# Two small matrix products moved to where fillers ran, with new orders for weight halves, a table load and PSUM banks

## The chip, the cores and the metric

The kernel runs on one core of one Trainium2 chip. The core's engines are TensorE (PE, matrix products), VectorE (DVE), ScalarE (ACT), GpSimd (POOL) and the queue SyncE (SP) that issues the DMAs. The metric is the device time of one execution in microseconds (us). Lower is better. The time of the kernel before is 937.57 us, the median of three runs.

## The reference

All of it is fp32. A first transformer block works on 16 meta tokens and 256 tokens of width 1024 (two kinds of attention, a feed-forward with a causal convolution of width 3), a second on the 256 tokens (differential attention, retention, a feed-forward). What matters here is the frame around the two norms of the first block and the end of the second:

```python
# first block
h = h + rms_norm(mixed, norm_gains[layer, 1])
xn = rms_norm(h, norm_gains[layer, 2])
u = causal_depthwise_conv(xn @ w_up[layer], conv_w[layer], conv_b[layer])
u_gate, u_val = jnp.split(u, 2, axis=-1)
ffn = (jax.nn.gelu(u_gate, approximate=True) * u_val) @ w_down[layer]
h = h + rms_norm(ffn, norm_gains[layer, 3])
# second block: p is 256 tokens x 256, w_ple 256 x 1024
x = x + mixed @ w_out[i]
h2 = rms_norm_2(x, g_mlp[i])
x = x + jnp.square(jax.nn.relu(h2 @ w_ff1[i])) @ w_ff2[i]
gate_p = jax.nn.sigmoid(rms_norm_2(x, g_ple[i]) @ w_ple_gate[i])
x = x + gate_p * (p[i] @ w_ple[i])
return rms_norm_2(x, g_final)
```

The product `p @ w_ple` needs nothing that the two blocks compute. It is the "per-layer input" product that the change moves.

## The kernel before

Activations lie transposed, 8 tiles of 128 features by the tokens. Each fp32 matrix product is made of three products of halves: a value is split in a high half (rounded) and a low half (the rest), and high times high, high times low and low times high are summed in PSUM.

All weights lie in DRAM as one list of 285 blocks of 128x1024 in order of use. SyncE loads block i into one of four `raw` slots. ScalarE's `hi_to` (L826) makes its high half `wh`, VectorE's `lo_to` (L1270) its low half `wl`, and TensorE uses the block. In one of eight blocks (i % 8 == 7) VectorE makes the high half too, with a CAST (L1266). Four slots mean that the halves of block i can be made once block i-4 is used. `hi_to(n)` and `lo_to(n)` make the halves up to block n-1 at the point at which they stand in the engine's program. Each engine runs its own program strictly in the order written, so where these calls stand decides what waits for what.

One block is one tile of 128 output features, 8 steps of 3 matmuls of 256 columns. `group` runs two or three tiles together, step by step, so that it can begin while the last steps of its input are still being made. `ple` multiplies p by w_ple: 2 blocks (B_PLE0, B_PLE1), 4 output tiles each, 24 matmuls a block. B_PLE0 stands between the output product `w_out_2` and the second feed-forward, B_PLE1 between that feed-forward and the gate product `w_ple_gate`. Their results are copied from PSUM by 8 activations (`ple_copy`, L1197). `warm(n, b)` issues n matmuls of ones by ones into a bank that nobody reads. They stand behind the sums of squares of two norms of the first block, where TensorE would wait for the residual.

A norm goes: squares, sum over the features by a matmul with ones, `root` on ScalarE (Ln L832, Exp L834), then on VectorE per feature tile the scaled value (L1496), the residual (L1505) and the low half of the next input (L1286), beside the high half (L988) and the square (L994) on ScalarE.

The first feed-forward runs 22 steps j. A step has two `up` tiles (gate and value half), whose products VectorE scales into `work` (L1537). ScalarE starts the convolution (L1018), VectorE ends it (L1548, L1552), ScalarE applies gelu (L1026, after a table load at j = 0), VectorE multiplies gate and value (L1558), and the product is split in halves for the `down` tile (`z_hi` L1005 on ScalarE, `z_lo` L1274 on VectorE). The first `down` tile follows the `up` tiles of the step 2.

The last gate runs its 8 tiles in 3 PSUM banks, so that tile 4 has to wait until VectorE has read the bank of tile 1 (L1834, the product with the norm's root).

## Time and profile before

| | |
|---|---|
| median of three runs | 937.57 us (937.49 to 938.95) |
| the profiled execution's own time | 940.0 us |
| its span | 938.7 us |
| mean granted TensorE clock | 0.997 |
| TensorE, VectorE, ScalarE busy | 98%, 71%, 51% |
| DMA | 165 GB/s on average |

The profile is one execution. Its span is what the engines' records cover; its own time is 1.3 us longer, and 2.4 us above the median of the three runs. Records start when an instruction begins on its engine. A bracket behind a record gives the idle time before it and the record on another engine that ended it. TensorE's matmuls overlap: what counts for their pace is the distance of their starts, not the length of one.

The names in a record are the program's: `wh`, `wl` and `raw` as above, `a1h`/`a1l` and `a2h`/`a2l` and `xnh`/`xnl` halves of activations, `hT` the residual, `qk`, `tmpb`, `work`, `gt`, `va` buffers, `rb` a norm's root, `bank` PSUM.

### The profile page before, as it was taken

Reading aid. Unit: us, or ns where it says so; the run is one execution under the profiler, and the core shown is the slowest. Engines: PE = TensorE matmul, PEld = TensorE weight load, DVE = VectorE, ACT = ScalarE, POOL = GpSimd, SP = SyncE. Lnnn points to the kernel's source line nnn. Section 1 sums busy time; section 2 is a strip of 40 time slices with the busy share of each in tenths; the row PEclk is TensorE's granted clock in tenths of the full one; section 3 lists DMA queues with packets and bytes.
Section 4 is the critical chain, followed back from the end, with each engine's and each line's share of the span. In section 5 each row is a group of like instructions: output and inputs, shape, how many; then the busy total and the mean of one; then the engine's idle time right before and its main releaser. Section 6 shows DMA issues by size and latency. Waiting matters only on the chain.

```text
span 938.7 us, 17949 instructions
## 1 busy us (share of the span) xinstructions
PE 920.1 (98%) x7270; PEld 883.6 (94%) x7270; DVE 668.9 (71%) x1170; ACT 481.3 (51%) x856; POOL 64.4 (7%) x125
## 2 busy tenths in 40 slices
PE   8999999999999999999999999999999999999997
PEld 7899988999999999998999988999999999999996
DVE  6654576578878778879699977786756665656666
ACT  5365354545654455466466643553346544444456
POOL 3112100122000000000000100000102000000002
PEclk9999999999999999999999999999999999999999
DMA  7543543544465555554544463665645665555641
GB/s 277 179 138 112 157 128 102 172 139 157 135 195 180 175 194 185 181 186 133 195 138 132 134 193 98 182 184 181 191 151 183 201 185 190 186 184 186 186 141 46
DMA packets 43170, 154.73 MB, mean 165 GB/s; under 512 B 4688, under 2 KB 6224, under 8 KB 42960
## 3 DMA queue, kind: packets, MB, share of 16 engines
q1 hardware_dynamic: 43088, 153.59, 51.2%
q8 instruction: 58, 0.95, 0.4%
q14 instruction: 24, 0.20, 0.1%
HBM read 152.52 MB, written 1.05 MB: 164 GB/s over the span
## 4 chain that ended last, share of the span: by engine, by line
PE 85%; DVE 8%; ACT 4%; issue 2%; DMA 0%; DVEq 0%; ACTq 0%
PE bank L243 84%; DVE wl L1270 3%; ACT wh L826 1%; ACT work L1062 1%; DVE work L1633 0%; DMA hT<-in_xT 0%; DVE a1l L1286 0%; DVE work L1631 0%; DVE wh L1266 0%; DVE tmpb L1840 0%; DVE work L1614 0%; ACT rb L832 0%; DVE tmpb L1834 0%; DVE hT L1817 0%; DVE tmpb L1552 0%
## 5 line engine op out<-in xcount | busy, mean ns | idle before, releaser
L1270 DVE TENSOR_TENSOR wl<-raw,wh 128x1024 fp32r<-128x1024 f32 x285 | 351.6, 1242 | 124.3 <-ACT wh L826 122.4
L826 ACT ACTIVATE wh<-raw 128x1024 fp32r<-128x1024 f32 x250 | 260.8, 1052 | 149.0 <-PE bank L243 147.0
L243 PE MATMUL bank<-a2h,wh 128*128 128x256 f32 x880 | 250.9, 286 | 4.1 <-DVE wl L1270 3.0
L243 PE MATMUL bank<-a2h,wl 128*128 128x256 f32 x880 | 247.8, 282 | 0.0
L243 PE MATMUL bank<-a2l,wh 128*128 128x256 f32 x880 | 245.6, 282 | 0.0
L243 PE MATMUL bank<-a1h,wh 128*128 128x258 f32 (+1 forms) x800 | 226.1, 284 | 1.9 <-DVE wl L1270 0.7
L243 PE MATMUL bank<-a1h,wl 128*128 128x258 f32 (+1 forms) x800 | 224.4, 282 | 0.0
L243 PE MATMUL bank<-a1l,wh 128*128 128x258 f32 (+1 forms) x800 | 219.9, 281 | 0.0
L243 PEld LDWEIGHTS bank<-a2h,wh 128*128 128x128 f32 x880 | 166.3, 189 | 7.6 <-issue 4.9
L243 PEld LDWEIGHTS bank<-a2h,wl 128*128 128x128 f32 x880 | 166.5, 189 | 0.0
L243 PEld LDWEIGHTS bank<-a2l,wh 128*128 128x128 f32 x880 | 165.3, 189 | 0.2
L243 PEld LDWEIGHTS bank<-a1h,wh 128*128 128x128 f32 x800 | 150.9, 189 | 3.0 <-issue 2.0
L243 PEld LDWEIGHTS bank<-a1h,wl 128*128 128x128 f32 x800 | 151.0, 189 | 0.1
L243 PEld LDWEIGHTS bank<-a1l,wh 128*128 128x128 f32 x800 | 149.3, 189 | 0.1
L243 PE MATMUL bank<-xnh,wh 128*128 128x258 f32 (+2 forms) x408 | 116.9, 288 | 0.0
L243 PE MATMUL bank<-xnh,wl 128*128 128x258 f32 (+2 forms) x408 | 114.7, 283 | 0.0
L243 PE MATMUL bank<-xnl,wh 128*128 128x258 f32 (+2 forms) x408 | 112.9, 283 | 0.0
L243 PEld LDWEIGHTS bank<-xnh,wh 128*128 128x128 f32 x408 | 76.8, 188 | 1.1 <-issue 0.2
L243 PEld LDWEIGHTS bank<-xnh,wl 128*128 128x128 f32 x408 | 76.9, 189 | 0.0
L243 PEld LDWEIGHTS bank<-xnl,wh 128*128 128x128 f32 x408 | 75.8, 189 | 0.1
L1018 ACT ACTIVATE tmpb<-work,ccol 128x256 f32<-128x256 f32 x44 | 26.5, 602 | 41.5 <-DVE work L1537 41.5
L1211 ACT ACTIVATE tmpb<-tmpb 128x256 f32<-128x256 f32 x32 | 13.3, 418 | 65.6 <-DVE tmpb L1795 65.6
(231 smaller groups left out, 1018.4 us busy)
## 6 DMA issues: line engine op xcount, KB each, us to landing
raw<-in_wts SPq DMA_DIRECT2D x285, 512.0 KB, 3.6
csb<-in_cst SPq DMA_DIRECT2D x1, 1428.0 KB, 10.8
hT<-in_xT SPq DMA_DIRECT2D x2, 544.0 KB, 4.5
out<-va SPq DMA_DIRECT2D x2, 512.0 KB, 2.9
qk<-in_pT SPq DMA_DIRECT2D x1, 256.0 KB, 3.9
gr<-in_lamv SPq DMA_DIRECT2D x1, 128.0 KB, 10.6
ccol<-in_fcst SPq DMA_DIRECT2D x1, 126.0 KB, 4.9
```

Of the source, the lines that this page charges most:

```text
L243: return e.matmul(o, lhsT, rhs, start=start, stop=stop, skip_group_check=True)
L826: e.activation(wh[:, i % NHL, :], raw[:, i % NRAW, :], ACT.Copy).then_inc(s_hi, 1)
L1018: e.activation(tmpb[:, slot, 0:S], work[:, (2 * j + half) % 8, 2:2 + S], ACT.Identity, bias=ccol[:, c + 3:c + 4], scale=ccol[:, c + 2:c + ...
L1062: e.activation(ee[:, a:b], ee[:, a:b], ACT.Exp, bias=nb[:, 2 * c + j:2 * c + j + 1], accum_out=sm[:, 2 * c + j:2 * c + j + 1]).then_inc(s_ ...
L1211: e.activation(x, x, ACT.Square).then_inc(s_zq, 1)
L1270: e.tensor_tensor(lo, src, hi.bitcast(F32), ALU.subtract).then_inc(s_lo, 1)
```

## The change

- The products with p move. B_PLE0 becomes block 57, ahead of the first feed-forward, and takes the place of `warm(12, 5)`. B_PLE1 becomes block 124, behind that feed-forward, and takes the place of `warm(12, 1)`. Nothing stands where they were. The halves of p lie in slots 4 and 5 of `a2h` and `a2l`, made in the stage of the first block's output products, and p's DMA goes with them, to `va`. The results are copied by 4 activations of 128x2x256 (`ple_out`, L1010) in place of 8 of 128x256. The second block's gates (GATE2) move to other buffers.
- The high halves that VectorE makes are those with i % 8 == 4.
- Orders: in both residual loops the halves of some blocks are made at other steps. In the feed-forward the gelu table is loaded behind the first conv activation, and the halves of the first down block are made earlier, as is `z_lo` of step 1. In the last step, the halves of the last input (`z_hi`, `z_lo`) come ahead of those of a block.
- Banks: the sum of the second norm goes to bank 4, the last output tile to bank 4, and the gate's 8 tiles to banks (1, 3, 4, 5, 7, 4, 5, 7). Its tiles 2 to 4 wait only for the residual.

```diff
-B_VB, B_VA, B_F, B_QKB, B_QKA, B_G, B_WO, B_WOUT, B_FF = 0, 4, 8, 9, 17, 25, 41, 49, 57
-B_V2 = B_FF + 3 * FF1
+B_VB, B_VA, B_F, B_QKB, B_QKA, B_G, B_WO, B_WOUT, B_PLE0, B_FF = 0, 4, 8, 9, 17, 25, 41, 49, 57, 58
+B_PLE1 = B_FF + 3 * FF1
+B_V2 = B_PLE1 + 1
...
+    return i + 1 - hid_count(i)
+def hid_count(i):
+    return (i + 4) // 8
...
-        GB, B_GS = (4, 5, 7), 6
+        GATE_BANK, B_GS = (1, 3, 4, 5, 7, 4, 5, 7), 6
...
+            def ple(i, m):
+
+                e.wait_ge(s_lo, i + 1)
+                s = i % NHL
+                for j in range(2):
+                    o = bank[PLE_BANK[m // 2]][:, j * S:j * S + S]
+                    for k in range(2):
+                        c = (2 * ((m + j) % 4) + k) * 128
+                        h, l = wh[:, s, c:c + 128], wl[:, s, c:c + 128]
+                        mm(o, h, ph(k), j == 0 and k == 0, False)
+                        mm(o, h, pl(k), False, False)
+                        t = mm(o, l, ph(k), False, k == 1)
+                return t
...
             e.wait_ge(s_mt, 6)
-            warm(12, 5)
-
+            e.wait_ge(s_pl, 2)
+            ple(B_PLE0, 0).then_inc(s_pt, 1)
+            e.wait_ge(s_mt, 7)
+            ple(B_PLE0, 2).then_inc(s_blk, 1)
...
-            warm(12, 1)
+            ple(B_PLE1, 4).then_inc(s_pt, 1)
+            ple(B_PLE1, 6).then_inc(s_blk, 1)
...
-            e.wait_ge(s_pl, 2)
-            for m in range(4):
-                e.wait_ge(s_x2, m + 2)
-                ple(B_PLE0, m, 1 + m)
...
-            for m in range(4, 8):
-                e.wait_ge(s_rl, FF2 - 7 + m)
-                ple(B_PLE1, m, m - 4)
...
             for m in range(2, 8):
-                if m == 2:
-                    e.wait_ge(s_x3, 8)
+                if m < 5:
+                    e.wait_ge(s_x3, 8 if m == 4 else 4)
                 else:
                     e.wait_ge(s_gq, m - 2)
...
-                    if i % 8 != 7:
+                    if i % 8 != 4:
...
             root(1, bank[7][:, 0:LQ], LQ, 1024)
-            hi_to(B_FF + 4)
...
+            def ple_out(q):
+                if q % 2:
+                    e.wait_ge(s_blk, (B_PLE1 if q > 1 else B_PLE0) + 1)
+                else:
+                    e.wait_ge(s_pt, q // 2 + 1)
+                e.activation(gt[:, 2 * q:2 * q + 2, 0:S], bank[PLE_BANK[q]][:, 0:512].rearrange("p (j n) -> p j n", j=2),
+                             ACT.Copy).then_inc(s_pp, 1)
...
             def residual_hi(n, n0, n1, gcol, dst):
                 for k in range(KT):
+                    if k == 3 and n == 0:
+                        hi_to(B_FF + 4)
+                    elif k == 4 and n == 1:
+                        hi_to(B_V2 + 4)
...
             residual_hi(0, T0, L, COL_G2, a1h)
+            ple_out(0)
+            ple_out(1)
             hi_to(B_FF + 5)
...
+                        if (j, half) == (0, 0):
+                            e.preload_act_table_set(GELU_SET)
...
-                if j >= LAG1:
+                if j >= LAG1 and j != FF1 - 1:
                     hi_to(down1(j - LAG1) + 4)
...
-            hi_to(B_V2 + 4)
+            hi_to(B_V2 + 3)
             residual_hi(1, NM, L, COL_GMIX, a2h)
+            ple_out(2)
+            ple_out(3)
...
-            hi_to(B_PLE0 + 4)
-            for m in range(4):
-                ple_copy(m, 1 + m)
+            hi_to(B_FF2 + 4)
             root(5, bank[7][:, 0:S], S, 1024)
...
                 if m == 5:
-                    hi_to(B_PLE1 + 4)
-            for m in range(4, 8):
-                ple_copy(m, m - 4)
-            hi_to(B_GP + 4)
+                    hi_to(B_GP + 4)
             root(6, bank[B_GS][:, 0:S], S, 1024)
...
+            lo_to(B_FF + 3)
+            add_normed(0, lambda k: qk[:, k, 0:LQ], COL_G1, rb[:, 1, 0:LQ], 2, T0, L, N_UP1, COL_G2, a1h, a1l, {6: B_FF + 4})
...
+                        if n == 2:
+                            z_lo(1, 0, tmpb[:, 1, 0:S])
...
-            lo_to(B_V2 + 3)
-            add_normed(1, FD, COL_G3, rb[:, 1, 0:S], 4, NM, L, N_IN2, COL_GMIX, a2h, a2l, B_V2 + 4, 5)
+            lo_to(B_V2 + 2)
+            add_normed(1, FD, COL_G3, rb[:, 1, 0:S], 4, NM, L, N_IN2, COL_GMIX, a2h, a2l, {3: B_V2 + 3, 6: B_V2 + 4})
```

Three places show how the engines' orders move. In the rows, a name with a number is a PSUM bank, and x2 or x4 means so many alike in a row. Line numbers of the changed kernel are higher: its L1287 is the low half of a block (L1270 before), L838 the high half (L826), L1291 is `z_lo` (L1274), L1559, L1572 and L1576 are the scaling and the convolution (L1537, L1548, L1552), L1582 gate times value (L1558).

First, VectorE at the start of the first feed-forward, from the tile of bank 1 to the halves of the first down block. Before:

```order
L1537 TENSOR_TENSOR work<-bank1,rb 128x258
L1270 TENSOR_TENSOR wl<-raw,wh 128x1024
L1548 SCALAR_TENSOR_TENSOR tmpb<-work,ccol,tmpb 128x256
L1552 SCALAR_TENSOR_TENSOR tmpb<-work,ccol,tmpb 128x256
L1537 TENSOR_TENSOR work<-bank2,rb 128x258
L1558 TENSOR_TENSOR tmpb<-tmpb 128x256
L1548 SCALAR_TENSOR_TENSOR tmpb<-work,ccol,tmpb 128x256
L1274 TENSOR_TENSOR a2l<-tmpb,a2h 128x256
L1552 SCALAR_TENSOR_TENSOR tmpb<-work,ccol,tmpb 128x256
L1537 TENSOR_TENSOR work<-bank3,rb 128x258
L1266 CAST wh<-raw 128x1024
L1270 TENSOR_TENSOR wl<-raw,wh 128x1024
```

And in the changed kernel:

```order
L1559 TENSOR_TENSOR work<-bank1,rb 128x258
L1287 TENSOR_TENSOR wl<-raw,wh 128x1024
L1572 SCALAR_TENSOR_TENSOR tmpb<-work,ccol,tmpb 128x256
L1576 SCALAR_TENSOR_TENSOR tmpb<-work,ccol,tmpb 128x256
L1559 TENSOR_TENSOR work<-bank2,rb 128x258
L1582 TENSOR_TENSOR tmpb<-tmpb 128x256
L1287 TENSOR_TENSOR wl<-raw,wh 128x1024
L1291 TENSOR_TENSOR a2l<-tmpb,a2h 128x256
L1572 SCALAR_TENSOR_TENSOR tmpb<-work,ccol,tmpb 128x256
L1576 SCALAR_TENSOR_TENSOR tmpb<-work,ccol,tmpb 128x256
L1559 TENSOR_TENSOR work<-bank3,rb 128x258
```

The CAST is gone, the low half of the down block (the second L1287 row) and `z_lo` stand ahead of the convolution of the third tile, not behind it.

Second, ScalarE at the end of the second norm, where the second block's values start. `a2h` is the high half of the next input, `qk<-hT` a square. Before:

```order
L988 ACTIVATE a2h<-hT,ccol 128x256
L994 ACTIVATE qk<-hT 128x256
L988 ACTIVATE a2h<-hT,ccol 128x256
L994 ACTIVATE qk<-hT 128x256
L826 ACTIVATE wh<-raw 128x1024 x4
L832 ACTIVATE rb<-bank2,ccol 128x256
L834 ACTIVATE rb<-rb 128x256
```

And in the changed kernel:

```order
L1003 ACTIVATE a2h<-hT,ccol 128x256
L1021 ACTIVATE qk<-hT 128x256
L1003 ACTIVATE a2h<-hT,ccol 128x256
L1021 ACTIVATE qk<-hT 128x256
L1010 ACTIVATE gt<-bank1 128x2x256
L1010 ACTIVATE gt<-bank2 128x2x256
L838 ACTIVATE wh<-raw 128x1024 x4
L844 ACTIVATE rb<-bank2,ccol 128x256
L846 ACTIVATE rb<-rb 128x256
```

The two copies of p's products now stand ahead of the four high halves.

Third, ScalarE at the last gate, from the last input tile over the root (`rb`) and the sigmoid table to the first sigmoid (`tmpb<-tmpb`). Before:

```order
L988 ACTIVATE a1h<-hT,ccol 128x256
L1220 ACTIVATE qk<-hT 128x256
L1197 ACTIVATE qk<-bank0 128x256
L1197 ACTIVATE qk<-bank1 128x256
L1197 ACTIVATE qk<-bank2 128x256
L1197 ACTIVATE qk<-bank3 128x256
L826 ACTIVATE wh<-raw 128x1024
L832 ACTIVATE rb<-bank6,ccol 128x256
L834 ACTIVATE rb<-rb 128x256
L1227 ACT_TABLE_LOAD
L826 ACTIVATE wh<-raw 128x1024
L1241 ACTIVATE tmpb<-tmpb 128x256
```

And in the changed kernel:

```order
L838 ACTIVATE wh<-raw 128x1024
L1003 ACTIVATE a1h<-hT,ccol 128x256
L1240 ACTIVATE qk<-hT 128x256
L1003 ACTIVATE a1h<-hT,ccol 128x256
L1240 ACTIVATE qk<-hT 128x256
L844 ACTIVATE rb<-bank6,ccol 128x256
L846 ACTIVATE rb<-rb 128x256
L1244 ACT_TABLE_LOAD
L838 ACTIVATE wh<-raw 128x1024
L1258 ACTIVATE tmpb<-tmpb 128x256
```

The four copies are gone, and the high half that stood behind them stands two input tiles earlier.

## Rows read from the trace of the kernel before

**Rows 1.** The page, part 1: busy time, share of the span, instructions.

```profile
PE 920.1 (98%) x7270; PEld 883.6 (94%) x7270; DVE 668.9 (71%) x1170; ACT 481.3 (51%) x856; POOL 64.4 (7%) x125
```

**Rows 2.** The page, part 4: the chain that ended last, by engine.

```profile
PE 85%; DVE 8%; ACT 4%; issue 2%; DMA 0%; DVEq 0%; ACTq 0%
```

**Rows 3.** Waits of TensorE: waited for, us in total, times, longest.

```profile
PE bank L243 <- DVE wl L1270: 3.7, 3, 2.1
```

**Rows 4.** Timeline (start us, us, engine line op) of TensorE: fillers and what follows.

```profile
223.84 2.84 PE L243 MATMUL bank<-onesb 128*128 128x128 f32 x24
...
226.91 0.36 PE L243 MATMUL bank<-a1h,wh 128*128 128x258 f32 x1 [0.23 <-ACT a1h L988]
...
425.78 2.84 PE L243 MATMUL bank<-onesb 128*128 128x128 f32 x24
```

**Rows 5.** Timeline of TensorE, first products of the feed-forward.

```profile
248.71 0.36 PE L243 MATMUL bank<-a2h,wh 128*128 128x256 f32 x1 [2.09 <-DVE wl L1270]
...
253.14 0.28 PE L243 MATMUL bank<-a1h,wh 128*128 128x258 f32 x1
```

**Rows 6.** Timeline of VectorE, around the first norm and the first halves.

```profile
225.00 0.89 DVE L1496 SCALAR_TENSOR_TENSOR tmpb<-qk,ccol,rb 128x258 f32<-128x258 f32 x2 [1.42 <-ACT rb L834]
...
246.62 0.68 DVE L1266 CAST wh<-raw 128x1024 fp32r<-128x1024 f32 x1
...
247.34 1.22 DVE L1270 TENSOR_TENSOR wl<-raw,wh 128x1024 fp32r<-128x1024 f32 x1
```

**Rows 7.** Windows: length, busy us of each engine, PEclk, DMA share, GB/s.

```profile
249.70:253.10 3.40, 3.40 (x18) 3.40 (x17) 3.31 (x8) 2.11 (x4) 0.00 (x0) 0.50 0.66 222
440.00:452.00 12.00, 12.00 (x55) 9.54 (x54) 6.99 (x10) 5.03 (x6) 0.00 (x0) 1.00 0.66 218
900.00:908.00 8.00, 8.00 (x69) 8.00 (x68) 7.65 (x22) 6.51 (x19) 0.00 (x0) 1.00 0.25 77
```

**Rows 8.** Timeline of ScalarE, around the gelu table load.

```profile
242.75 1.28 ACT L1025 ACT_TABLE_LOAD   x1
244.04 0.42 ACT L1026 ACTIVATE tmpb<-tmpb 128x256 f32<-128x256 f32 x1
```

**Rows 9.** Timeline of all engines, last down tile of the first feed-forward.

```profile
420.26 0.42 DVE L1274 TENSOR_TENSOR a2l<-tmpb,a2h 128x256 fp32r<-128x256 f32 x1
...
420.73 0.39 PE L243 MATMUL bank<-a2h,wh 128*128 128x256 f32 x1 [1.07 <-DVE a2l L1274]
```

**Rows 10.** Timeline of all engines, where the second set of values starts.

```profile
437.11 2.00 ACT L826 ACTIVATE wh<-raw 128x1024 fp32r<-128x1024 f32 x2
...
437.33 0.69 DVE L1266 CAST wh<-raw 128x1024 fp32r<-128x1024 f32 x1
...
440.10 0.40 PE L243 MATMUL bank<-wh,a2h 128*128 128x512 f32 x1
```

**Rows 11.** Groups by form: a ScalarE copy of 512 PSUM columns.

```profile
L1254 ACT ACTIVATE va<-bank,small 128x512 f32<-128x512 f32 x2 | 1.3, 685 | 0.0
```

**Rows 12.** Timeline of TensorE, p products ahead of the second feed-forward.

```profile
714.29 0.47 PE L243 MATMUL bank<-xnh,wh 128*128 128x256 f32 x1
...
717.59 0.47 PE L243 MATMUL bank<-a1h,wh 128*128 128x256 f32 x1
```

**Rows 13.** Timeline of all engines, around the last gate.

```profile
903.22 0.29 PE L243 MATMUL bank<-a1h,wh 128*128 128x256 f32 x1
...
907.31 0.48 DVE L1286 SCALAR_TENSOR_TENSOR a1l<-hT,ccol,a1h 128x256 fp32r<-128x256 f32 x1
...
909.80 0.36 PE L243 MATMUL bank<-a1h,wh 128*128 128x256 f32 x1 [0.68 <-DVE wl L1270]
...
912.47 0.47 ACT L832 ACTIVATE rb<-bank,ccol 128x256 f32<-128x256 f32 x1 [2.92 <-PE bank L243]
...
914.70 1.06 ACT L826 ACTIVATE wh<-raw 128x1024 fp32r<-128x1024 f32 x1
...
917.41 0.39 PE L243 MATMUL bank<-a1h,wh 128*128 128x256 f32 x1 [0.34 <-DVE tmpb L1834]
```

More of the change, by code:

```diff
@@ L225, in program @@
         VR_BANK = ((0, 1), (2, 5))
-        W_OUT_BANK = lambda m: m % 7
-        ph = lambda k: xnh[:, k, 0:S]
-        pl = lambda k: xnl[:, k, 0:S]
+        W_OUT_BANK = lambda m: m if m < 7 else 4
+        p_in = va[:, 0, :].rearrange("p (k t) -> p k t", k=2)
+        ph = lambda k: a2h[:, 4 + k, :]
+        pl = lambda k: a2l[:, 4 + k, :]
+        PLE_BANK = (5, 6, 1, 2)
         r_ret = lambda h: work[:, 4 * (h % 2) + 1, 0:S]
@@ L738, in tensor_engine, with up2_sum @@
                     mm(bank[7][:, 0:S], ones, qk[:, 3 + 6 % 4, 0:S], False, False)
-            def ple(i, m, b):
-                t = tile(i, bank[b][:, 0:S], ph, pl, [2 * (m % 4), 2 * (m % 4) + 1], kx=[0, 1])
-                t.then_inc(s_blk if m % 4 == 3 else s_pt, 1)
-            e.wait_ge(s_pl, 2)
-            for m in range(4):
-                e.wait_ge(s_x2, m + 2)
-                ple(B_PLE0, m, 1 + m)
-            e.wait_ge(s_sqa, 36 + 8)
-            mm(bank[7][:, 0:S], ones, qk[:, 3 + 7 % 4, 0:S], False, True).then_inc(s_sum, 1)
-            e.wait_ge(s_x2, 8)
-            e.wait_ge(s_pp, 1)
-            group(B_FF2, [bank[b][:, 0:S] for b in range(2)], 0, S, N_UP2, A1[0], A1[1])
+            def up2_sum(k):
+                if k == 3:
+                    e.wait_ge(s_sqa, 36 + 8)
+                    mm(bank[7][:, 0:S], ones, qk[:, 3 + 7 % 4, 0:S], False, True).then_inc(s_sum, 1)
+            e.wait_ge(s_x2, 2)
+            group(B_FF2, [bank[b][:, 0:S] for b in range(2)], 0, S, N_UP2, A1[0], A1[1], after=up2_sum)
             for j in range(FF2 + LAG2):
@@ L969, in scalar_engine @@
                 hi_to(B_WO + m + 4)
+                if m == 6:
+                    e.wait_ge(s_p, 16)
+                    for k in range(2):
+                        e.activation(ph(k), p_in[:, k, :], ACT.Copy).then_inc(s_ph, 1)
                 if m >= 2:
@@ L996, in scalar_engine @@
             residual_hi(0, T0, L, COL_G2, a1h)
+            ple_out(0)
+            ple_out(1)
             hi_to(B_FF + 5)
-            root(2, bank[6][:, 0:LQ], LQ, 1024)
+            root(2, bank[4][:, 0:LQ], LQ, 1024)
             hi_to(B_FF + 6)
@@ L1177, in scalar_engine @@
             hi_to(B_WOUT2 + 5)
-            e.wait_ge(s_p, 16)
-            for k in range(2):
-                e.activation(ph(k), qk[:, k, 0:S], ACT.Copy).then_inc(s_ph, 1)
             for m in range(9):
@@ L1472, in vector_engine @@
                 lo_to(B_WO + m + 4)
+                if m == 7:
+                    for k in range(2):
+                        e.wait_ge(s_ph, k + 1)
+                        low(pl(k), p_in[:, k, :], ph(k)).then_inc(s_pl, 1)
                 if m >= 2:
@@ L1766, in vector_engine @@
                 e.wait_ge(s_gs, RAW_GATES + 8 + m + 1)
-                mix(N_MIX2, m, S, bank[(2 * m) % 8][:, 0:S], bank[(2 * m + 1) % 8][:, 0:S])
+                mix(N_MIX2, m, S, bank[(2 * m) % 8][:, 0:S], bank[(2 * m + 1) % 8][:, 0:S], GATE2(m), GATE2(8 + m))
             mix_lo(N_MIX2, 7, a2h, a2l)
             lo_to(B_WOUT2 + 5)
-            for k in range(2):
-                e.wait_ge(s_ph, k + 1)
-                low(pl(k), qk[:, k, 0:S], ph(k)).then_inc(s_pl, 1)
             for m in range(9):
```

89 lines of the change are left out of this document (40 added, 49 removed).

## The prediction

> **What bounds the kernel.** I read the busy shares first: TensorE is busy 98% of the span [rows 1], 18.6 us short of all of it. Then the chain of waits: 85% of it is TensorE, 8% VectorE, 4% ScalarE [rows 2]. So a matmul that goes is time that goes, if what it covered does not come out as a wait, and a wait of TensorE that goes is time as well. The table of TensorE's waits names the first candidate, the low halves of weight blocks, 3.7 us in 3 waits, the longest 2.1 [rows 3]. Last I read the timeline around each of the five places that the change touches. My working moves the rows of those places by hand.
>
> **The products with p, as a whole.** They are 2 x 24 matmuls and cost the same wherever they run. In both places where they land stand 24 filler matmuls of 2.84 us [rows 4], 0.118 us each, and matmuls of 256 columns go at the same pace. So nothing is added there on TensorE and 2 x 2.84 = 5.7 us of its work go from the places where they stood. What follows is what the five places give back or add.
>
> **1. First norm to the first down tile (after block 57).** VectorE gets a CAST (0.68) and a low half (1.22 long, 1.14 to the next start) ahead of the residual loop. It waited 1.42 us there [rows 6], so 0.69 + 0.03 + 1.14 = 1.86 pushes the loop by 0.4. The group that started at 226.91, right behind its high half [rows 4], starts at 227.3. Later in the stage VectorE does less ahead of the first down tile: the CAST (0.72 to the next start) is gone, and the convolution of the third tile with its scaling (0.40 + 0.40 + 0.34 by the starts of such rows) has moved behind. That is 1.86 us, and with the table load, which now comes while VectorE works on the tile of bank 1, I get the low half ready at about 246.7. Down 0 starts there instead of at 248.71 [rows 5], 2.0 earlier. What is late next is the low half of the block behind it: VectorE now does the moved convolution and another half, up to 251.15, so TensorE waits 1.6 us and then 0.3 at the next block. Against this stands what before lost in the same stretch: the clock was granted at 0.50 for 3.40 us behind the wait of 2.09 us [rows 7], so that down 0 took from 248.71 to 253.14, 4.43 us [rows 5] where 24 matmuls at 0.118 take 2.84. If it isn't granted low again, the stage ends **1.6 earlier**: -2.0 (start of down 0) - 1.6 (clock) + 1.9 (new waits) = -1.7, and 0.1 for the pipeline's filling at two more starts. The bounds are 0 (the clock falls again) and -2.1.
>
> The table load took 1.28 us and the next activation started 0.01 us behind it [rows 8]. The Trainium skill, ScalarE: Activation LUTs, section "What ACT_TABLE_LOAD costs", adds a drain to the load, about 2.7 us together. By the page the second convolution of the step would come some 1.4 us later and this term would be nearer to -0.7. I go by the row.
>
> **2. End of the first feed-forward.** The last down tile starts at 420.73 after 1.07 us of waiting for the low half of its input, and VectorE made that half at 420.26, behind a weight half [rows 9]. In the new order ScalarE takes z_hi right after the table load, and VectorE has z_lo done at about 419.2. Of the 1.2 us the chain of squares and adds behind the tile takes back 0.1: **-1.1** (0 to -1.3).
>
> **3. Second norm to the second set of values.** Here the trace speaks against the change. Block V2+4 has its high half made by VectorE at 437.33, while ScalarE starts on the next at 437.11, and TensorE wants the block at 440.10 [rows 10]. After the change the high half is ScalarE's, and it stands behind two more things: one more low half in VectorE's residual loop, which delays ScalarE's last input tile by about 1.1 us to 438.3, and two copies of 512 PSUM columns. A ScalarE copy of that form took 0.685 [rows 11], 0.55 to 0.6 to the next start. So the high half runs 439.4 to 440.4 and the low half to 441.7: TensorE waits 1.6 us that it didn't wait, **+1.6**. Bounds: +0.4, if the loop is no longer than before (437.1 + 1.15 + 1.0 + 1.2 = 440.5, against 440.10), or below that down to 0 if the values' start moves too, and +2.2, if a copy is as long as 0.685 twice over and the loop two low halves longer.
>
> **4. w_out_2 to the second feed-forward.** Between 714.29 and 717.59 stand 24 products with p and one last sum [rows 12]. The sum (0.24) stays, as it only moves in between the group's matmuls. 3.3 - 0.24 = 3.06 goes. The group needs a second block's low half and the eighth input tile. VectorE loses the low halves of p and a CAST in front of w_out_2, and gets another CAST in its loop, so up to 0.4 us could come on top (the 0.95 us wait is one of the three in [rows 3]) or go. **-3.1** (-2.4 to -3.5).
>
> **5. Second feed-forward to the gate.** 24 matmuls (2.84) go ahead of 903.22 [rows 13]. But the group of the gate's first tiles cannot end 2.84 earlier. VectorE was busy 7.65 us of the 8 in 900 to 908 [rows 7], and makes the last input's low half at 907.31. So the group starts at 901.0 and ends at 908.2. The wait of 0.68 at 909.80 goes, as the CAST and four copies do. The sum comes 1.6 earlier, the root starts at 910.8 instead of 912.47, the high half of a block at 913.05 instead of 914.70, and its low half is done at 915.4. Tile 4 started at 917.41, behind VectorE's read of a bank; with more banks it doesn't wait for that, but for this low half, at 915.4: **-2.0** (-1.0 to -2.8).
>
> **Costed at nothing.** p's DMA goes to the w_o stage, its four small halves (0.4 each) too, where VectorE and ScalarE have slack. The other moved CASTs, one of eight blocks as before, fall at other tiles of both attentions: 0, with 0.5 either way, since each of their chains alternates between three engines.
>
> **Sum.** -1.6 - 1.1 + 1.6 - 3.1 - 2.0 = -6.2. The profiled execution took 940.0 with a span of 938.7, so it would take 933.8 with a span of 932.5. Its own time lies 2.4 above the median of the runs; from 937.57 the same sum gives **931.4 us**.
>
> **The rivals.**
> A. The clock is granted low again at a new wait, the 1.6 us one in place 1 or the one in place 3. For it: before, it fell behind a wait of 2.09 us. Against: the wait of 1.07 us [rows 9] and the others brought next to nothing, since the mean clock of the execution was 0.997, and 3.40 us at half of it already take 0.002. My new waits lie between. Price 1.6 each: 933.0, both 934.6. The Trainium skill, TensorE: Matmul & The Clock Gate, section "HAM oscillation — how this bites in real kernels", tells of matmuls in chunks that restart at the lower clock behind waits for data, which is what the rows show here once.
> B. The wait of place 3 is short, as the loop was waiting in part already and takes its extra low half without getting longer: 931.4 - 1.2 = 930.2. For it: the 1.1 us by which I let the loop grow is no row, it is where I put the low half between other records. Against: even so 0.4 is left, by the lower bound above.
> C. The removed p products hid VectorE's chains, and their removal shows as waits. Place 5 then gives 0 in place of -2.0 and place 4 half, 1.5 less: 931.4 + 3.5 = 934.9. For it: the 7.65 us of 8 in [rows 7]. Against: in place 4 before, TensorE reached the group with its first inputs long made.
> D. Slower: the wait of place 3 brings the low clock, and waits at each following block keep it low through the rest of the values. Those are 12.00 us of busy TensorE, 440 to 452 [rows 7], and at half the clock 12.0 more: 943.4. It decides against the change once over 6.2 us of matmuls run at half the clock there. Against it: the one low stretch in the trace lasted 3.40 us.
>
> **Chances.** My forecast 0.55, A 0.17, B 0.09, C 0.12, D 0.04, and 0.03 for something that I don't see and that takes the gain back. A measurement of this kernel tells about 0.2% (1.9 us) from no change. Under 935.7 lie the forecast, B, nearly all of A and most of C: 0.88. Within 0.2%: 0.07. Over 939.4: 0.05. The range is 929.3 to 935.0: below it a sum with B and place 4 at its better bound, above it D and the worst of A and C together.
>
> **What would show it.** Right: 48 matmuls on xnh gone, 24 with a2h in each place of the fillers; down 0 starting some 2 us earlier relative to the stage's start, with waits of 1.6 and 0.3 behind it; PEclk at 1.00 there; the last down tile with under 0.3 us of wait; a new wait for a low half of some 1.6 us in the second set of values; the second feed-forward's group right behind w_out_2's sums; gate tile 4 waiting for a low half, not for tmpb. The prediction fails if a low clock stretch of over 4 us appears, if place 3 costs over 3 us, or if places 4 and 5 together give under 3 us.

## The result and the profile after

The changed kernel takes 935.54 us (median of 10 runs, 935.31 to 936.67), the kernel before 937.63 us in the same series (10 runs, 937.49 to 939.81). The ratio is 0.9971, with a 95% interval of 0.9963 to 0.9980. So the change makes the kernel 2.1 us faster. Forecast were 6.2 us, 931.4 with a range of 929.3 to 935.0: the sign was right, the size three times too large. The times of the kernel before stand in two groups with a gap of 1.7 us, about half of the executions in each (more on this at the experiments). Seven of these ten lie in the lower group, so 2.1 is the gain over that one; over the upper one it is 3.7.

The profiled execution of the changed kernel took 935.41 us, about its median, with a span of 934.2, 4.5 less than the span before. The page's parts 1 and 4, to be put beside [rows 1, 2]:

```profile
PE 912.8 (98%) x7222; PEld 874.7 (94%) x7222; DVE 668.3 (72%) x1171; ACT 479.3 (51%) x851; POOL 57.7 (6%) x125
...
PE 85%; DVE 9%; ACT 3%; issue 2%; DMA 1%; SPq 0%; DVEq 0%; ACTq 0%
```

TensorE has 7.3 us less of busy time and the span is only 4.5 us shorter: the rest came out as waits. The table of TensorE's waits (columns as in [rows 3]) shows some of them:

```profile
PE bank L249 <- issue: 3.1, 4, 1.3
PE bank L249 <- DVE wl L1287: 2.3, 3, 1.2
PE bank L640 <- DVE work L1659: 0.9, 1, 0.9
```

Low halves (L1287) are waited for 2.3 us and not 3.7, but waits put down to "issue" are now 3.1 us. At 438.46, the longest of these, VectorE had just ended a low half (below, at place 3), so the name says only that the trace did not tell the releaser. Then there are the five places, on TensorE's timeline:

```profile
226.82 0.36 PE L249 MATMUL bank<-a1h,wh 128*128 128x258 f32 x1 [0.42 <-ACT a1h L1003]
...
246.40 0.36 PE L249 MATMUL bank<-a2h,wh 128*128 128x256 f32 x1
...
250.69 0.36 PE L249 MATMUL bank<-a1h,wh 128*128 128x258 f32 x1 [1.21 <-DVE wl L1287]
...
422.43 0.47 PE L249 MATMUL bank<-a2h,wh 128*128 128x256 f32 x1
...
438.46 0.47 PE L249 MATMUL bank<-wh,a2h 128*128 128x512 f32 x1 [1.35 <-issue]
...
725.45 0.28 PE L249 MATMUL bank<-a2h,wh 128*128 128x256 f32 x1
...
911.63 0.36 PE L249 MATMUL bank<-a1h,wh 128*128 128x256 f32 x1 [0.47 <-DVE wl L1287]
```

The reader can lay each beside its row of before and take the difference of the starts, as in this table. What a stage gave is the change of the difference from one line to the next.

| point | before | after | before less after | gain of the stretch |
|---|---|---|---|---|
| first values | 12.16 | 11.30 | 0.86 | 0.86, not the change |
| behind the first wait of the attention | 54.02 | 53.84 | 0.18 | -0.68 |
| first up tiles [rows 4] | 226.91 | 226.82 | 0.09 | -0.09 |
| down 0 [rows 5] | 248.71 | 246.40 | 2.31 | 2.22 |
| tile behind down 0 [rows 5] | 253.14 | 250.69 | 2.45 | 0.14 |
| down 1 | 258.92 | 256.77 | 2.15 | -0.30 |
| fillers or p products [rows 4] | 425.78 | 422.43 | 3.35 | 1.20 |
| second set of values [rows 10] | 440.10 | 438.46 | 1.64 | -1.71 |
| end of the differential attention | 534.15 | 533.19 | 0.96 | -0.68 |
| first down tile of the second feed-forward | 729.18 | 725.45 | 3.73 | 2.77 |
| gate tile 4 [rows 13] | 917.41 | 911.63 | 5.78 | 2.05 |
| output DMA | 934.86 | 930.30 | 4.56 | -1.22 |

The first line isn't the change: before_63 below, the kernel before with one CAST less, has its first values at 11.15, and banks_old, the changed kernel with other banks, has them at 12.08.

The rows of before in it that no group has yet:

```profile
1.12 4.21 PE L243 MATMUL bank<-onesb 128*128 128x128 f32 x18 [1.12 <-DVE onesb L1289]
5.89 3.99 PE L243 MATMUL bank<-qk,onesb 128*128 128x272 f32 x8 [0.57 <-DVE qk L1296]
9.68 1.80 PE L243 MATMUL bank<-onesb 128*128 128x128 f32 x10
12.16 0.47 PE L243 MATMUL bank<-wh,xnh 128*128 128x512 f32 x1 [0.68 <-ACT xnh L838]
...
54.02 0.39 PE L243 MATMUL bank<-xnh,wh 128*128 128x258 f32 x1
...
258.92 0.28 PE L243 MATMUL bank<-a2h,wh 128*128 128x256 f32 x1
...
534.15 0.36 PE L243 MATMUL bank<-a2h,wh 128*128 128x256 f32 x1
...
729.18 0.28 PE L243 MATMUL bank<-a2h,wh 128*128 128x256 f32 x1
...
934.86 0.98 SPq L1940 DMA_DIRECT2D out<-va  x2
```

And those of after:

```profile
5.82 3.21 PE L249 MATMUL bank<-qk,onesb 128*128 128x272 f32 x8 [1.07 <-DVE qk L1313]
8.87 1.28 PE L249 MATMUL bank<-onesb 128*128 128x128 f32 x10
11.30 0.47 PE L249 MATMUL bank<-wh,xnh 128*128 128x512 f32 x1 [1.15 <-ACT xnh L850]
...
52.84 1.08 PE L249 MATMUL bank<-qk,gr 64*128 64x258 f32 x12 [0.62 <-issue]
53.84 0.39 PE L249 MATMUL bank<-xnh,wh 128*128 128x258 f32 x1
...
256.77 0.28 PE L249 MATMUL bank<-a2h,wh 128*128 128x256 f32 x1
...
533.19 0.37 PE L249 MATMUL bank<-a2h,wh 128*128 128x256 f32 x1
...
930.30 0.98 SPq L1959 DMA_DIRECT2D out<-va  x2
```

In a window around the stretch in which the clock was low before, it is now at full speed (columns as in [rows 7]):

```profile
240.00:262.00 22.00, 20.79 (x171) 20.39 (x170) 20.22 (x37) 14.38 (x24) 0.00 (x0) 1.00 0.55 169
```

The loss of the last line of the table is seen on VectorE, at the last block's halves:

```profile
917.27 0.69 DVE L1283 CAST wh<-raw 128x1024 fp32r<-128x1024 f32 x1
917.99 1.71 DVE L1287 TENSOR_TENSOR wl<-raw,wh 128x1024 fp32r<-128x1024 f32 x1
919.62 0.41 DVE L1854 TENSOR_TENSOR tmpb<-bank,rb 128x256 f32<-128x256 f32 x1
```

The CAST and a low half of 1.71 us stand between a gate tile's product and the next read of a bank. Before, ScalarE made that high half.

### The profile page after: what moved, and what is told of

The parts are those of the page before. It is cut to its first block, busy times and chain, and to the rows that moved or that the text cites. A ratio compares the mean times of both kernels' runs of the same rounds, so it can differ in the third digit from the quotient of the medians.

```text
span 934.2 us, 17836 instructions
## 1 busy us (share of the span) xinstructions
PE 912.8 (98%) x7222; PEld 874.7 (94%) x7222; DVE 668.3 (72%) x1171; ACT 479.3 (51%) x851; POOL 57.7 (6%) x125
## 3 DMA queue, kind: packets, MB, share of 16 engines
HBM read 152.52 MB, written 1.05 MB: 164 GB/s over the span
## 4 chain that ended last, share of the span: by engine, by line
PE 85%; DVE 9%; ACT 3%; issue 2%; DMA 1%; SPq 0%; DVEq 0%; ACTq 0%
PE bank L249 84%; DVE wl L1287 3%; ACT wh L838 1%; DMA raw<-in_wts 1%; DVE work L1659 0%; DVE wh L1283 0%; ACT work L1095 0%; DVE work L1640 0%; DVE hT L1861 0%; DVE tmpb L1576 0%; DVE work L1657 0%; DVE tmpb L1859 0%; DVE a1l L1303 0%; DVE tmpb L1572 0%; DVE tmpb L1854 0%
## 5 line engine op out<-in xcount | busy, mean ns | idle before, releaser
L1287 DVE TENSOR_TENSOR wl<-raw,wh 128x1024 fp32r<-128x1024 f32 x285 | 353.4, 1248 | 130.1 <-ACT wh L838 128.4
L838 ACT ACTIVATE wh<-raw 128x1024 fp32r<-128x1024 f32 x249 | 259.6, 1052 | 147.2 <-PE bank L249 139.1
L249 PE MATMUL bank<-a2h,wh 128*128 128x256 f32 x896 | 255.0, 285 | 0.6 <-DVE wl L1287 0.6
L249 PE MATMUL bank<-a2h,wl 128*128 128x256 f32 x896 | 251.6, 282 | 0.0
L249 PE MATMUL bank<-a2l,wh 128*128 128x256 f32 x896 | 249.5, 281 | 0.0
L249 PE MATMUL bank<-xnh,wh 128*128 128x258 f32 (+2 forms) x392 | 112.3, 288 | 0.0
L249 PE MATMUL bank<-xnh,wl 128*128 128x258 f32 (+2 forms) x392 | 110.2, 283 | 0.0
L249 PE MATMUL bank<-xnl,wh 128*128 128x258 f32 (+2 forms) x392 | 108.4, 283 | 0.0
L249 PEld LDWEIGHTS bank<-xnh,wh 128*128 128x128 f32 x392 | 73.8, 188 | 1.1 <-issue 0.2
L249 PEld LDWEIGHTS bank<-xnh,wl 128*128 128x128 f32 x392 | 73.9, 189 | 0.0
L249 PEld LDWEIGHTS bank<-xnl,wh 128*128 128x128 f32 x392 | 72.8, 189 | 0.0
L1291 DVE TENSOR_TENSOR a2l<-tmpb,a2h 128x256 fp32r<-128x256 f32 x62 | 26.3, 424 | 27.3 <-ACT a2h L1034 25.1
## 6 DMA issues: line engine op xcount, KB each, us to landing
csb<-in_cst SPq DMA_DIRECT2D x1, 1428.0 KB, 10.8
```

What stands on the lines that cost most here:

```text
L249: return e.matmul(o, lhsT, rhs, start=start, stop=stop, skip_group_check=True)
L838: e.activation(wh[:, i % NHL, :], raw[:, i % NRAW, :], ACT.Copy).then_inc(s_hi, 1)
L1287: e.tensor_tensor(lo, src, hi.bitcast(F32), ALU.subtract).then_inc(s_lo, 1)
L1291: return e.tensor_tensor(lo, src, hi.bitcast(F32), ALU.subtract)
```

## The experiments

Each is compared with the changed kernel (935.54) or the kernel before. The changed kernel itself was timed in the first series only. The experiments ran in four later ones, each on another chip, with the kernel before beside them. Its lowest time was 937.3 to 937.4 in three of these and 937.7 in the one of table_old, so differences of under some 0.3 us between series tell nothing.

One gap ran through all: the times of the kernel before stand in groups. In one series of 27 runs, 12 lay from 937.38 to 937.84 and 15 from 938.84 to 939.91. In the four series together it has 94 runs, 47 below 938.3 (median 937.59) and 47 above 938.8 (median 939.25). The mean granted clock goes with the group: 0.998 in 44 of the 47 lower ones, 0.995 to 0.997 in all of the upper ones. Its median falls in either group by chance, so I read groups and profiles, and not medians alone.

**before_again: the kernel before once more.** No edit.

> The kernel before, unchanged, for a second profile. My theory (profile sample): the execution profiled before was 2.4 us above its median because of two things that its usual executions lack, a start 0.86 us later and the low clock of 3.4 us behind the wait at 248.71, which cost 1.6 us. Then this profile takes 937.5 to 938, with PEclk 1.00 from 240 to 262 or a span of 936.3, and down 0 to the next tile takes 2.9 us, not 4.4. Rival (always there): the low clock is a property of this wait; it shows again, and the 2.4 us have another source. Time ratio 1.000 in either case.

It took 939.16 (11 runs, 937.44 to 939.90), its profiled execution 939.86. The wait and the low clock are in the profile again:

```profile
248.61 0.36 PE L243 MATMUL bank<-a2h,wh 128*128 128x256 f32 x1 [2.09 <-DVE wl L1270]
...
253.05 0.28 PE L243 MATMUL bank<-a1h,wh 128*128 128x258 f32 x1
```

```profile
249.70:253.10 3.40, 3.40 (x21) 3.40 (x20) 3.31 (x8) 2.21 (x4) 0.00 (x0) 0.61 0.77 234
```

Down 0 took 4.44 us, and PEclk was 0.61. So this second profile was no typical execution either; it belongs to the upper group, as the first one. My theory that a second profile would lack it missed, and what follows the wait in an execution of the lower group had to be shown otherwise.

**before_63: the kernel before, without the CAST in front of the first down tile.**

```diff
+def by_dve(i):
+    return i % 8 == 7 and i != B_FF + 6
-                    if i % 8 == 7:
+                    if by_dve(i):
```

> The kernel before, but ScalarE makes the high half of the first down block (63), not VectorE. Theory (the two groups of times of the kernel before, 937.5 and 939.1, are this wait without and with the low clock behind it): the CAST's 0.72 us go, TensorE waits about 1.35 us and not 2.09, the clock stays at 1.00 behind it and the times are one group near 936.8. Rival: the low clock comes from elsewhere or from any wait over 1 us: two groups 1.5 us apart stay, both 0.7 lower.

It took 936.80, as expected, and the 11 runs form one group: ten from 936.66 to 937.02 and one at 937.75. The wait is 1.36 us and the clock stays:

```profile
11.15 0.47 PE L253 MATMUL bank<-wh,xnh 128*128 128x512 f32 x1 [1.16 <-ACT xnh L848]
...
247.11 0.36 PE L253 MATMUL bank<-a2h,wh 128*128 128x256 f32 x1 [1.36 <-DVE wl L1280]
```

```profile
249.50:253.00 3.50, 3.50 (x31) 3.50 (x31) 3.38 (x8) 3.00 (x5) 0.00 (x0) 1.00 0.63 187
```

The upper group is gone. With the profiles of the two executions of before, both from the upper group and both with the low stretch, and with the mean clocks of all runs, this shows that the groups of the kernel before are this wait without and with the low clock behind it: 1.6 us in the profile, 1.7 between the groups' medians. No profile caught an execution of the lower group.

A rival is the late start, which both of those profiles have too (12.16 and 12.11, against 11.15 here). It is worth 0.9 and not 1.7, and ff1_old (next) has the low stretch with an early start, so it doesn't make the groups. It comes on top: 937.6 + 1.6 + 0.9 = 940.1, and the two profiled executions took 940.0 and 939.9, at the upper end of their group.

**ff1_old: the old orders in the first feed-forward.**

```diff
-                        if (j, half) == (0, 0):
-                            e.preload_act_table_set(GELU_SET)
...
+                        e.preload_act_table_set(GELU_SET)
                     e.activation(g, g, ACT.Gelu_apprx_tanh).then_inc(s_gl, 1)
...
-                        if n == 2:
-                            z_lo(1, 0, tmpb[:, 1, 0:S])
...
+            hi_to(B_FF + 3)
```

The CASTs of the blocks 57 to 123 stood at i % 8 == 0, and the early halves at `B_FF + 7` were out.

> The changed kernel, but the start of the first feed-forward in the old order: the gelu table loaded ahead of gelu, the halves of the first down block and z_lo of step 1 where they were, the CASTs of this feed-forward at the old tiles (that of the first down block again). Theory: TensorE waits some 2 us before down 0 again, and behind it the clock is granted low in part of the runs: times in two groups 1.5 us apart, the better one 0 to 0.5 us slower than the changed kernel, as the new order only trades one wait of 2.1 for waits of 0.3 to 1.4; median 935.6 to 937. Rival: the new order is worth its 2 us by itself: one group at 937.5.

It took 939.28, 3.7 more than the changed kernel and above the 935.6 to 937 that I expected. Part of it is my edit: with no CAST at block 60, ScalarE had to make its high half before the residual, and a wait of 2.15 appeared in front of the first up tiles. So the test is no pure reversal. What it does show is a second kernel with groups. The runs stand at 937.83, at 939.08 to 939.57 (seven) and at 940.84 to 941.20 (three). There are now two waits over 2 us:

```profile
228.46 0.36 PE L254 MATMUL bank<-a1h,wh 128*128 128x258 f32 x1 [2.15 <-ACT a1h L1009]
...
250.25 0.36 PE L254 MATMUL bank<-a2h,wh 128*128 128x256 f32 x1 [2.09 <-DVE wl L1291]
```

```profile
228.50:232.00 3.50, 3.50 (x26) 3.38 (x27) 3.50 (x10) 3.19 (x8) 0.00 (x0) 1.00 0.30 117
251.00:253.00 2.00, 2.00 (x11) 2.00 (x11) 2.00 (x5) 0.74 (x2) 0.00 (x0) 0.50 0.74 246
```

In this execution (939.08, of the middle group) the clock stayed behind the first wait and fell behind the second. That the lowest run had neither fall and the three upper ones both is likely by their mean clocks (0.997, and 0.992 to 0.994), but no profile shows it.

**table_old: only the table load moved back.**

```diff
-                        if (j, half) == (0, 0):
-                            e.preload_act_table_set(GELU_SET)
...
                     if j == 0:
+                        e.preload_act_table_set(GELU_SET)
```

In the second place it stands ahead of gelu.

> The changed kernel, but the gelu table is loaded directly ahead of the first gelu as before; the other orders of the first feed-forward stay. Theory (term 1 of the prediction counts the load as hidden once it moves): the load of 1.28 us comes back between the second convolution and gelu, the product of step 0 and with it z_hi and z_lo come 0.5 to 1.3 us later, and down 0 starts that much later: 0.5 to 1.0 us slower than the changed kernel. Rival: what brought down 0 forward is the order on VectorE and the CAST that left, and the load hides behind them anyway: 0 to 0.3 slower.

936.55 (9 runs, 936.00 to 936.85), 1.0 slower, of which some 0.2 is the series: the kernel before was that much slower in it too. Down 0 waits 0.65 us for its input's low half:

```profile
247.31 0.36 PE L249 MATMUL bank<-a2h,wh 128*128 128x256 f32 x1 [0.65 <-DVE a2l L1291]
```

From the first up tile (227.01 here) to down 0 it is 20.30 us, against 19.58 in the changed kernel (226.82 to 246.40). So of the 2.2 us by which down 0 comes earlier, 0.7 is the load's place. The CAST alone is worth 0.8, by before_63 (226.10 to 247.11, 21.01, against 21.80 before). If the parts add, the order of the halves brought the other 0.7.

**cast_fox, cast_diff, cast_tail: which blocks' high halves VectorE makes.** Each changes one line of the changed kernel:

```diff
-                    if i % 8 == 4:
+                    if i % 8 == (7 if i < B_PLE0 else 4):            # cast_fox
+                    if i % 8 == (1 if B_V2 <= i < B_WOUT2 else 4):   # cast_diff
+                    if i % 8 == 4 and i < N_BLOCKS - 1:              # cast_tail
```

> The changed kernel, but blocks 0 to 56 (the first block's attention and both output products) have their high halves made by VectorE for i % 8 == 7, as before, and not 4. Theory (casts cost): the 4.5 us between the profiles hide a loss of 0.42 us up to the first norm, by the CASTs of blocks 12 and 36: 0.3 to 0.5 us faster than the changed kernel (935.1), the wait of 0.6 us at 52.8 gone. Rival: the attention's start depends on the csb transfer, not on the CAST, and nothing changes: 935.5.

935.36 (8 runs). The first up tiles start at 226.48 and not 226.82, and the wait at 52.8 is gone from the trace. Counted from the first values (11.41 here, 11.30 in the changed kernel) the gain at the up tiles is 0.45. The median moved by 0.2 only; the span of the profiled execution is 934.3, as the last matmuls of this one ran at the low clock (from 926.7 on, where the changed kernel had full clock up to 929.0). So the trace shows the expected gain, and in the times it is inside the noise.

> The changed kernel, but among the blocks of the second block's attention, retention and gates (V2 up to w_out_2) VectorE makes the high halves of those with i % 8 == 1, which are the places that it had before, block V2+4 among them. Theory (casts cost): 0.6 us come back between 480 and 535, where the wait at 532 was 1.01 and before 0.63, and some 0.7 at V2+4, as VectorE makes that half itself while ScalarE copies: 1.2 to 1.4 us faster than the changed kernel (934.2). Rival: only place 3 improves, and the attention's loss is not the CASTs': 934.8.

934.32 (5 runs, 934.32 to 934.56), 1.2 faster. Both waits shrink, from 1.35 and 0.85. Counted from the first values (11.16 here), 1.05 us come at place 3 and 0.4 at the end of the differential attention (531.61), of the 0.68 lost there:

```profile
437.27 0.47 PE L254 MATMUL bank<-wh,a2h 128*128 128x512 f32 x1 [0.26 <-issue]
...
531.30 0.33 PE L645 MATMUL bank<-csb,work 128*128 128x128 f32 x1 [0.27 <-DVE work L1664]
```

> The changed kernel, but the high half of the last block (284) is made by ScalarE and not by VectorE. Theory (tail is VectorE's chain): from the last gate tile's start to the end took 12.06 us before and 13.39 after, by the CAST of 0.69 and a low half of 1.71 at 917.3 to 919.7: 1.0 to 1.4 us faster than the changed kernel (934.3). Rival: the tail is as long as ScalarE's chain of sigmoids, squares and scaled values, which now gets 1.05 us more: 935.5 or slower.

934.76 (9 runs, 934.31 to 936.03), 0.8 faster, and 1.0 by the lowest runs of each. In the profile TensorE's last sums start 15.66 us behind gate tile 4 (911.68), against 16.65 in the changed kernel, so 1.0 of the tail's 1.2 came back. Then the clock, low from 926.8 on here and from 929.0 in the changed kernel, took 0.5 of it: from these sums to the output DMA it is 2.50 us here and 2.02 there. The sums here, then those of the changed kernel:

```profile
927.34 1.01 PE L254 MATMUL bank<-onesb,qk 128*128 128x1 f32 x4 [1.55 <-ACT qk L1254]
...
928.28 0.61 PE L249 MATMUL bank<-onesb,qk 128*128 128x1 f32 x4 [1.55 <-ACT qk L1249]
```

**v2_first: the high half of block V2+4 ahead of the copies.**

```diff
                     elif k == 4 and n == 1:
                         hi_to(B_V2 + 4)
+                    elif k == 7 and n == 1:
+                        hi_to(B_V2 + 5)
```

> The changed kernel, but ScalarE makes the high half of block V2+4 before the last input tile of the second norm, ahead of that tile's halves and the two copies of p's products. Theory (place 3 as predicted): TensorE's wait at 436.9 to 438.46 is for that block's low half, which will start at 435.4 and end at 436.6: 1.3 to 1.5 us faster than the changed kernel (934.1). Rival: TensorE waits for the copies (bank 2 and the eight inputs) as well, or the input tile comes later by ScalarE's 1.05 us and takes it back: 0 to 0.5 us faster.

933.77 (5 runs, 933.68 to 934.20), 1.8 faster, a little over the 1.3 to 1.5 expected. The set starts at 436.80 with no wait in front of it, 1.6 earlier when counted from the first values (11.22 here):

```profile
436.32 0.64 PE L249 MATMUL bank<-wh,a2l 128*128 128x512 f32 x2
436.80 0.39 PE L249 MATMUL bank<-wh,a2h 128*128 128x512 f32 x1
```

**banks_old and fill_gate: the two halves of place 5.**

```diff
# banks_old
-        GATE_BANK, B_GS = (1, 3, 4, 5, 7, 4, 5, 7), 6
+        GATE_BANK, B_GS = (4, 5, 7, 4, 5, 7, 4, 5), 6
+            e.wait_ge(s_x3, 4)
-                if m < 5:
-                    e.wait_ge(s_x3, 8 if m == 4 else 4)
+                if m == 2:
+                    e.wait_ge(s_x3, 8)
# fill_gate
             e.wait_ge(s_rl, FF2)
+            warm(12, 0)
             group(B_GP, ...)
```

> The changed kernel, but the last gate runs in 3 PSUM banks as before, with their waits. Theory: tile 4 waited 0.47 us for a low half at 911.63; with 3 banks it also waits for VectorE's read, which can only start behind the root: 0.3 to 0.8 us slower than the changed kernel (936.0). Rival: the root's path bounds it anyway and the banks bring nothing: 935.5.

937.62 (11 runs), 2.1 slower, but in two groups: 935.55 to 935.84 (three) and 936.95 to 938.04 (eight). The group of the first two tiles now has to wait until VectorE has added up the banks 4 and 5, and the clock falls behind that wait (before, the products with p stood in front of this group, and it had no wait):

```profile
899.77 0.35 PE L249 MATMUL bank<-a1h,wh 128*128 128x256 f32 x1 [2.12 <-DVE hT L1838]
...
914.51 0.39 PE L249 MATMUL bank<-a1h,wh 128*128 128x256 f32 x1 [0.34 <-DVE tmpb L1855]
```

```profile
902.00:904.00 2.00, 2.00 (x11) 2.00 (x10) 1.90 (x6) 2.00 (x6) 0.00 (x0) 0.50 0.00 0
```

The profiled execution is of the upper group and, as those of before, has the late start (first values at 12.08) as well. The three lower runs have a mean clock of 0.997, the eight upper ones 0.994 to 0.996. So without the low clock the old banks cost 0.0 to 0.2 us (medians, lowest runs), with it about 2. The wait of my expectation, for VectorE's read at tile 4, is there (0.34) but is not what costs.

> The changed kernel with 12 filler matmuls (2.84 us) where the second half of the products with p stood before, between the second feed-forward and the last gate. Theory (place 5 as predicted): the gate's first group waited 0.59 for its first input and 0.62 for its last, so 1.2 us of the 2.84 were hidden: 1.6 to 1.9 us slower than the changed kernel (937.3). Rival C: VectorE's chain bounds this place and the fillers cost under 0.5 us: 935.9.

`warm(12, 0)` shows in the trace as 24 matmuls. 936.13 (11 runs, 935.82 to 937.39), 0.6 slower. The group starts at 899.27, 1.9 later, tile 4 only 0.6 later, with the same wait for the same low half:

```profile
912.24 0.36 PE L249 MATMUL bank<-a1h,wh 128*128 128x256 f32 x1 [0.47 <-DVE wl L1288]
```

That is the mechanism of rival C: in the changed kernel 2.84 us of matmuls at this place cost 0.6, and 2.2 of them hide behind VectorE's chain. Its price, a place that gives nothing, didn't come. If the products with p hid as much before, the 2.05 us of place 5 are their 0.6, the banks' 0.2 at most (or 2 with the clock) and, for the rest, what the missing CAST and four copies and the earlier sum brought, which no run here parts.

**fill_ff2: fillers at place 4.**

```diff
+            e.wait_ge(s_x2, 4)
+            warm(12, 3)
             group(B_FF2, ...)
```

> The changed kernel with 12 filler matmuls (2.84 us) between the last output product and the second feed-forward, where the other half of the products with p stood. Theory (place 4 as predicted): nothing hides there, 2.5 to 2.9 us slower than the changed kernel, 938.2. Rival C: VectorE's and ScalarE's chains bound the place as they do at the gate, and the fillers cost under 1 us: 936.3.

938.38 (11 runs, 937.89 to 939.39), 2.84 slower than 935.54, the fillers' length; that it agrees to the last digit is luck. In the profile the group starts at 716.15 and not 713.42, 2.8 later when counted from the first values (11.26 here). Nothing was hidden there.

**best1 and best2: the parts together.** best1 is the changed kernel with the CASTs of cast_fox, those of cast_diff from V2+8 on, that of cast_tail, and v2_first. best2 adds:

```diff
-                            hi_to(i + 4)
+                            hi_to(i + (5 if (j, half) == (1, 1) else 4))
...
-                lo_to(B_FF + 6 if n == 1 else i + 4)
+                lo_to(B_FF + 6 if n == 1 else i + 5 if n == 3 else i + 4)
```

> The changed kernel with the CASTs at i % 8 == 7 up to block 56, at i % 8 == 1 from V2+8 to w_out_2 and at 4 elsewhere, none for the last block, and the high half of block V2+4 made by ScalarE ahead of the last input tile. Theory (the parts add): 0.3 (cast_fox) + 0.6 (attention) + 1.0 (tail) + 1.8 (v2_first) = 3.7 us faster than the changed kernel, 931.8. Rival: the parts share the same gain (v2_first moves the attention's wait as well): 932.8.

> best1, and the halves of the block behind the first down block are made one tile earlier on both engines. Theory: TensorE's wait of 1.21 us at 250.69 in the changed kernel is for a low half that VectorE starts 1.1 us after it could: 0.8 to 1.1 us faster than best1, 930.9. Rival: the convolution behind it comes later, and the wait appears at down 1: same as best1.

best1 took 932.42 (5 runs, 931.93 to 933.30), 3.1 of the 3.7 expected, between theory and rival. In the profiles, counted from the first values (11.19 here), the attention gave 0.4 and not 0.6 (it ends at 530.68), and the tail from gate tile 4 (909.13) to the output DMA (927.31) gave 0.5 and not 1.0, with the clock low from 924.3 on. best2 took 931.61 (5 runs, 931.43 to 931.97), 0.8 less, and 0.9931 [0.9918, 0.9943] of the kernel before. The wait of 1.21 behind down 0 is gone, but one of 0.89 stands a tile later, so the rival was half right:

```profile
252.80 0.36 PE L254 MATMUL bank<-a1h,wh 128*128 128x258 f32 x1 [0.89 <-DVE wl L1294]
```

Against the changed kernel every part of best1 and best2 is an order or a choice of engine; no work left the kernel.

## Why the prediction was wrong

**The step that failed** is the one headed "Costed at nothing", together with the last sentence of the sum.

First, the sum was made against the profiled execution and then taken off the median. It held 1.6 us of low clock (place 1). The profiled execution had this stretch, but an execution of 937.5 hasn't: before_63 and the mean clocks show that the groups are this stretch. I had noted that the profiled execution lay 2.4 us over the median and did not ask which 2.4 us they were. They are 1.6 of clock, visible in [rows 7], and 0.86 of a later start, which only a second profile shows. Taken off, the forecast would have been 6.2 - 1.6 = 4.6 us faster, 932.9. The table's first line is in no part of the change either; it is where the other 0.86 of the spans' 4.5 stems from. The term isn't empty: about half of the executions of before pay for the stretch, and those get it back.

Second, "the other moved CASTs: 0, with 0.5 either way". Measured in the table: -0.68 up to 54 us (cast_fox takes that wait away), -0.68 in the differential attention, -1.22 in the tail. With the 0.27 won elsewhere in the first attention (from 0.18 to 0.45 at w_out) that is 2.3 us. By the profiles cast_fox gave 0.45 of it back, cast_diff 0.4 (and 1.05 of place 3) and cast_tail 1.0. So some 1.8 of the 2.3 are shown to be the CASTs; what made the other 0.5, in the differential attention and the tail, stays open. My reason for the 0, that the chains alternate between three engines, counted against it: in both attentions the loss has just the length of a CAST. And I had not costed the last block at all; in the tail VectorE is itself the path, and the low half behind the CAST took 1.71 us and not 1.22, which no run explains. 4.6 - 2.3 = 2.3 us, and the measurement gave 2.1. Either slip alone would have left the time inside my range (933.0 or 933.7); together they give 935.3.

The other steps, one by one:

- **Place 1** (-1.6): the difference stood at 0.45 at the first tile of w_out (199.50 and 199.05), fell to 0.09 by the CAST and the low half in front of the first up tiles, and stood at 2.15 at down 1: 1.7 us gained. Right in the profile; without the 1.6 of clock it is 0.1 in the median. The start of down 0 was forecast 2.0 earlier and came 2.2 earlier; the new wait was forecast 1.6 and was 1.21; the low clock did not come in the profile, and the ten times form no second group (rival A is out). On the table load the row was right: the load ended at 241.88 and the next activation started at 241.99. The drain of the Trainium skill, ScalarE: Activation LUTs, section "What ACT_TABLE_LOAD costs", would have put it 1.4 us later.
- **Place 2** (-1.1): measured 1.2, from 2.15 at down 1 to 3.35 at the fillers.
- **Place 3** (+1.6): measured 1.7, with the wait of 1.35 at the block that I named. That the cause is the high half that moved to ScalarE behind the copies, v2_first and cast_diff show from both sides. VectorE made the low half at 437.13, behind ScalarE's copies and its high half:

```profile
435.08 1.06 ACT L1010 ACTIVATE gt<-bank 128x512 f32<-128x512 f32 x2
436.04 2.95 ACT L838 ACTIVATE wh<-raw 128x1024 fp32r<-128x1024 f32 x3
...
437.13 2.36 DVE L1287 TENSOR_TENSOR wl<-raw,wh 128x1024 fp32r<-128x1024 f32 x2 [1.74 <-ACT wh L838]
```

- **Place 4** (-3.1): measured 2.8, and 2.84 by fill_ff2.
- **Place 5** (-2.0): measured 2.05. The size was right and its parts were not: I let the group end with VectorE's chain, which is right (fill_gate), but put the rest down to the banks, and these cost at most 0.2 when undone, if the clock stays.
- **Rival C** did not come: place 5 gave 2.05 and not 0, place 4 gave 2.8. Its mechanism holds at place 5 (2.2 of 2.84 us hidden) and not at place 4; the sum had it in already. **Rival B** would have needed a short wait at place 3, **rival D** a low clock behind it; neither was there.

The start, 0.86 us earlier or later, is TensorE's clock too. The first 18 fillers of before take 4.21 us, 0.234 each, twice the 0.118 of the later ones. The trace's own clock records begin with the full clock at 10.0 to 10.8 us in the three profiles with a late start (before, before_again, banks_old: first values at 12.08 to 12.16), and at 4.0 to 7.3 us in the twelve others (11.15 to 11.41). PEclk says 1.00 in front of the first record as well, so it doesn't show this; the 8 matmuls ahead of the ten fillers do, with 3.99 us late and 3.21 early.

What stays open: why the clock comes late in some executions, and why it falls in some executions and not in others behind the same wait. Three of the four profiles with the low stretch have the late start and none of the eleven others has; whether the two belong together no run here tells.

## What to carry to other kernels

When the profiled execution is slower than the median, find which rows make the difference before anything is added up, since a term that only lives in slow executions is no gain for the median. A rule like "one in eight" that moves work between engines is a change at every place at which it lands: walk through those places, and those where three engines take turns and the tail first. And products that vanish in front of a chain on another engine are worth what remains of them once the chain is laid beside them; fillers of the same length in their place measure it in one run.

## What the runs showed of the hardware

Behind a wait of TensorE of 2.09 to 2.12 us the granted clock fell to 0.50 for 3.4 us in part of the executions, in three kernels (before, ff1_old, banks_old), at 250 and at 902 us. The times of these kernels stood in groups with gaps of 1.4 to 2.1 us. In ff1_old's profile it stayed at 1.00 behind a wait of 2.15, and behind waits of 1.21, 1.35 and 1.36 us it stayed in every profile. A sudden second group in the times of one kernel was here a wait just over 2 us. The Trainium skill, TensorE: Matmul & The Clock Gate, section "HAM oscillation — how this bites in real kernels", describes such falls between chunks of matmuls; the trace agrees on the fall, with waits shorter than those told of there.

In the tail, where TensorE has only sums and transposes between waits, the clock fell in every profile, at 924 to 936 us. Where it fell ahead of the last sums these took 1.01 us and not 0.61, and the output came 0.5 us later (cast_tail against the changed kernel).

ScalarE's table load took 1.28 us and the next activation followed after 0.01 [rows 8]; the drain that the Trainium skill, ScalarE: Activation LUTs, section "What ACT_TABLE_LOAD costs", adds to it did not show.
